# A gated linear-attention decoder block on eight cores: decay moved from k to the state, the gate pipeline started earlier, a weight scaled in slices, and another order for the last token block

## The chip, the cores and the metric

The kernel runs on the 8 cores of one Trainium2 chip. Each core computes one of the 8 batch entries with its own copy of all weights; the cores do not exchange data. The metric is the device time in microseconds of the slowest core.

Each core has a matrix engine (TensorE, PE in the profile, its weight loads PEld), a vector engine (VectorE, DVE), an activation engine (ScalarE, ACT), a general engine (GpSimd, POOL) and a queue engine (SyncE, SP). Every engine works through its own list of instructions strictly in the order of that list. It goes on to the next one when the semaphores that this one waits for have been raised.

## The reference

For x of 2048 tokens by 1024 channels per core:

```python
h = x @ W_in            # split: q 512 | k 512 | v 1024 | g 1024 | a_low 16 | u 1024 | z 1024 | gate_a 1024 | gate_b 1024
# branch A: gated linear attention, 4 heads, key width 128, value width 256
log_a = log_sigmoid(a_low @ w_gate_up + b_gate) / 16
S_t = diag(a_t) S_{t-1} + k_t^T v_t ;  o_t = q_t S_t        # computed chunk by chunk
y_a = rms_norm_per_head(o) * gn_w * silu(g)
# branch B: causal trailing means over 2, 4, 8, 16 tokens, minus the token, a per-group linear map
y_b = (pool(u) @ pool_w + pool_b) * pool_scale * silu(z)
merged = sigmoid(gate_a) * (y_a @ W_a) + sigmoid(gate_b) * (y_b @ W_b)
out = layer_norm(2**0.25 * x + merged @ W_o) * ln_w + ln_b
```

In chunk form, with b the running sum of log_a inside a chunk of 128 tokens and b_last its last value, k enters the state as k * exp(b_last - b), and the state is multiplied by exp(b_last) from chunk to chunk.

## The kernel before

The program is written out by hand: Python calls `PE(...)`, `ACT(...)`, `DVE(...)`, `POOL(...)` append one instruction each to that engine's list, with the buffers that it reads and writes; waits follow from these buffers. So the order of the calls is the order on each engine. Activations are kept transposed (channels on the 128 partitions, tokens along the row), in four token blocks `tb` of 512. A projection group is 8 matmuls of 128x512 into one of 8 PSUM banks, which another engine then empties ("evacuates").

The stages, with their time in the profile:

1. 0 to 41 us, head: `head_group` makes q and k of token block 0 and q of block 1, 32 matmuls each, k-slice by k-slice as the weights land. `mid` hooks put other work between the k-slices: the low-rank gate input of block 0 (`al_mm`) and the first two steps `a1_pre`.
2. 41 to 82 us, fill: the other 20 groups of q and k (`proj_qk`, L409), interleaved with the gate pipeline. The 16 units u are 4 token blocks times 4 heads. `a1_pre(u)` is one gate matmul (L369) and Exp and Ln on ACT (L372, L374). `a1_scan(u)` is a running sum over a chunk on DVE (L378). `a1_cum(u)` is three Exp on ACT (L385, L387, L389), which give exp(b), exp(-b) and exp(b_last), the last of these named `eblast`. When the four units of a block are done, `finalize_one` multiplies q by exp(b) and k by exp(-b) in place on DVE (L446, L448), and on POOL k by `eblast` into a second array `kdT` (L450). `drain_fin` issues one such unit at a time.
3. 82 to 248 us, attention: 32 iterations n, that is 16 chunks c times 2 head pairs hp. Between projection groups of v and g (`proj_vg`, L533, which use the two banks 2 and 3 in turn) stand the steps of the chunk: `st_T1S` (transposes of `kdT`, L549, and scores, L554), `st_UO1` (the chunk's contribution to the state, L571, and the output inside the chunk, L576), `st_O2` (output from the state, L588), `st_state` (DVE updates the state in float32, L604, and ACT makes a bfloat16 copy, L607), `st_sq` (sums of squares on ACT and POOL), `st_y` (DVE, L627), `st_Y` (transposes, L638). The queue of `drain_fin` goes on in the first iterations. At n = 8 `scale_w` multiplies the weight `wa0` by a column factor, one DVE instruction over 128x4096 (L258); at three later places it does so for `wa1`, `wb0` and `wb1`.
4. 248 to 464 us: gate a with W_a (`gate_piece`, L663 and L671), the pooling branch (L755, L797, scans on DVE), z (L838).
5. 464 to 639 us, last stage: `d_piece(g, dc)` makes one 128-channel piece of gate b with W_b for a token group g (matmuls L899 and L907, Sigmoid on ACT L903, product and sum on DVE L911, L913). `e_half` makes half of a 128-token tile of the output product (8 matmuls, L954), adds the residual on DVE with a row sum (L963), and takes the sum of squares on ACT (L969). Mean and variance are then made by small DVE instructions (L980, L982, L987) and one power on POOL (L990), and two DVE passes over 128x1024 (`n1` L996, `n2` L1003) normalise. The token groups are 512, 512, 512, 384 and 128; the pieces of the 128-token group are done in pairs (`d_pair`, L935). The list `order` sets how pieces and tiles follow one another; tile 15 is written out by hand after it.

SP issues the loads of x and the stores of the output; POOL issues the weight loads.

Of the kernel before, what the change touches and what calls it, by code (L numbers as in the profile page):

```python
# [7 lines left out]
F32 = mybir.dt.float32  # L8
# [127 lines left out]
def build_program():  # L136
# [35 lines left out]
    with ExitStack() as es:  # L172
# [157 lines left out]
        kdT = A4[:, 0:8192].rearrange("p (h t) -> p h t", h=4)  # L330
# [11 lines left out]
        b_kdb = [[Buf() for _ in range(4)] for _ in range(4)]  # L342
# [132 lines left out]

        head_group(0, 0, 1, 0, mid={4: al0_a, 7: al0_b})
        head_group(1, 0, 0, 4, mid={1: pre01})
        head_group(0, 1, 0, 0)
        al_blk(1)
        fill = [(kind, h, tb) for kind, tb in ((1, 1), (0, 2), (1, 2), (0, 3), (1, 3)) for h in range(4)]  # L480
        for u in range(NT):
# [5 lines left out]
            if u % 4 == 0:  # L487
# [3 lines left out]
            drain_fin(1)  # L491
# [3 lines left out]
        drain_fin(1)  # L495
# [47 lines left out]
        def st_T1S(n):  # L543
# [49 lines left out]
        def st_state(n):  # L593
# [4 lines left out]
            for j in range(2):  # L598
# [92 lines left out]
        for n in range(NS):  # L691
# [21 lines left out]
            if n == 8:  # L713
                scale_w(wa0, cols16[:, 0:8])
# [6 lines left out]
        if True:  # L721
# [7 lines left out]
            st_y(NS - 1)  # L729
            st_Y(NS - 2)  # L730
# [124 lines left out]
        if True:  # L855
# [16 lines left out]
            st = [(small2, small)[s // 2][:, (s % 2) * 16:(s % 2 + 1) * 16] for s in range(NSL)]  # L872
            Q = [slice(i * 256, (i + 1) * 256) for i in range(4)]
# [5 lines left out]
            groups = [(0, 512), (512, 512), (1024, 512), (1536, 384), (1920, 128)]  # L879
# [37 lines left out]
            def ld_xr(t):  # L917
                s = t % 3
                P.add("sp", lambda e: e.dma_start(out=xt[s], in_=x[t * 128:(t + 1) * 128, :]),
                      writes=b_xt[s], lane=f"xt{s}", extra=lasts)  # L920

            N_, V_, R_ = 8, 9, 10

            def d_pair(p):
                s = sctr[0] % 2
                sctr[0] += 1
                o, n = groups[4]
                banks = [next_bank(), next_bank()]
                for i in range(2):
                    for a in range(2):  # L930
                        m = (2 * p + a) % 4
                        W, wB = (gbw, wbw)[i][p // 2]
                        for k in range(KC):
                            rhs = xT[:, 3, k, 384:512] if i == 0 else szT[:, k, o:o + n]
                            PE(lambda e, i=i, a=a, m=m, W=W, k=k, rhs=rhs: e.matmul(  # L935
                                pb[banks[i]][:, a * 128:(a + 1) * 128], W[:, k, m * 128:(m + 1) * 128], rhs,
                                start=(k == 0), stop=(k == KC - 1)),
                               r=[wB] + ([b_sz[k][3]] if i else []), w=[bb[banks[i]]])
                    if i == 0:
                        ACT(lambda e: e.activation(sgm[s][:, 0:256], pb[banks[0]][:, 0:256], AF.Sigmoid),  # L940
                            r=[bb[banks[0]]], w=[b_sgm[s]])
                DVE(lambda e: e.tensor_tensor(tmpf[s][:, 0:256], pb[banks[1]][:, 0:256], sgm[s][:, 0:256], ALU.mult),
                    r=[bb[banks[1]], b_sgm[s]], w=[b_tmpf[s]])
                dst = maT[:, 2 * p:2 * p + 2, o:o + n]
                DVE(lambda e: e.tensor_tensor(dst, tmpf[s][:, 0:256].rearrange("p (a t) -> p a t", a=2), dst, ALU.add),
                    r=[b_tmpf[s]], w=b_mg[4][2 * p:2 * p + 2])

# [218 lines left out]
```

How the kernel before makes its waits and increments, by code:

```python
    def replay(self, eng_name, eng, sems):  # L108
        waited = {}
        for op in self.ops[eng_name]:
            need = {}
            for d in op.deps:
                if need.get(d.lane, 0) < d.ticket:
                    need[d.lane] = d.ticket
            for lane, val in need.items():
                if waited.get(lane, 0) < val:
                    eng.wait_ge(sems[lane], val)
                    waited[lane] = val
            ins = op.fn(eng)
            if op.sig:
                assert ins is not None
                ins.then_inc(sems[op.lane], 16 if op.is_dma else 1)
```

## Time and profile before

| | us |
|---|---|
| median of 3 runs | 640.21 (639.96 to 640.48) |
| the profiled execution | 640.21 |
| its span on the slowest core, core 4 | 638.7 |
| PE busy | 612.0 (96%), 3207 matmul records |
| DVE busy | 368.0 (58%) |
| ACT busy | 246.6 (39%) |
| POOL busy | 86.0 (13%) |

The profiled execution lasted 1.51 us longer than the span of its slowest core, and it equals the median of the runs. The chain of work that ended last lies on PE for 88% of the span, on DVE for 5%. PE's duration of a matmul includes its latency, so consecutive matmuls overlap; what a group costs is read from the start of one group to the start of the next.

### The profile page before, as it was taken

Reading aid. Unit: us, or ns where it says so; the run is one execution under the profiler, and the core shown is the slowest. Engines: PE = TensorE matmul, PEld = TensorE weight load, DVE = VectorE, ACT = ScalarE, POOL = GpSimd, SP = SyncE. Lnnn points to the kernel's source line nnn. Section 1 sums busy time; section 2 is a strip of 40 time slices with the busy share of each in tenths; the row PEclk is TensorE's granted clock in tenths of the full one; section 3 lists DMA queues with packets and bytes.
Section 4 is the critical chain, followed back from the end, with each engine's and each line's share of the span. In section 5 each row is a group of like instructions: output and inputs, shape, how many; then the busy total and the mean of one; then the engine's idle time right before and its main releaser. Section 6 shows DMA issues by size and latency. Waiting matters only on the chain.

```text
span 638.7 us, 9893 instructions; the slowest of 8 cores (635.6 to 638.7 us)
## 1 busy us (share of the span) xinstructions
PE 612.0 (96%) x3207; PEld 301.3 (47%) x3268; DVE 368.0 (58%) x621; ACT 246.6 (39%) x560; POOL 86.0 (13%) x141
## 2 busy tenths in 40 slices
PE   5999979999999999899999999999999999999995
PEld 1344335555555554444445544444444444445553
DVE  0148966676565642242123598394934666667787
ACT  0348955656656663211112433433331222222233
POOL 9003552132211212000000000001000000000010
PEclk7999989999999999999999999999999999999998
DMA  7999526000000001946102100005953113233342
GB/s 111 173 168 169 90 33 102 1 1 2 1 2 2 2 1 30 154 82 104 29 1 30 37 2 1 1 0 91 164 112 131 67 66 133 81 117 132 112 154 99
DMA packets 11569, 44.43 MB, mean 70 GB/s; under 512 B 1792, under 2 KB 2560, under 8 KB 8960
## 3 DMA queue, kind: packets, MB, share of 16 engines
q0 software_dynamic: 5904, 25.89, 25.2%
q1 hardware_dynamic: 5472, 17.65, 8.0%
q8 instruction: 27, 0.44, 0.3%
q14 instruction: 22, 0.18, 0.1%
q10 hardware_dynamic: 144, 0.26, 0.1%
HBM read 61.30 MB, written 8.39 MB: 109 GB/s over the span
## 4 chain that ended last, share of the span: by engine, by line
PE 88%; DVE 5%; issue 3%; DMA 3%; POOL 1%; ACT 0%; DVEq 0%; ACTq 0%; POOLq 0%
PE pb L533 16%; PE pb L663 9%; PE pb L838 9%; PE pb L671 9%; PE pb L797 9%; PE pb L954 9%; PE pb L899 8%; PE pb L907 8%; PE pb L409 3%; DMA ws<-head 3%; PE pb L430 2%; DVE A L378 1%; PE pb L935 1%; PE pb L755 1%; PE pb L576 1%
## 5 line engine op out<-in xcount | busy, mean ns | idle before, releaser
L533 PE MATMUL pb<-A,xT 128*128 128x512 bf16 x368 | 88.8, 385 | 2.8 <-DVE A L537 2.0
L676 DVE TENSOR_TENSOR A<-pb,sgm_t 128x512 bf16<-128x512 f32 x32 | 22.1, 691 | 85.8 <-PE pb L671 73.3
L663 PE MATMUL pb<-xT,ws 128*128 128x512 bf16 x251 | 60.0, 379 | 0.3
L899 PE MATMUL pb<-xT,ws 128*128 128x512 bf16 (+1 forms) x255 | 57.0, 366 | 0.1
L907 PE MATMUL pb<-A 128*128 128x512 bf16 (+1 forms) x252 | 56.7, 366 | 0.2
L838 PE MATMUL pb<-xT,ws 128*128 128x512 bf16 x251 | 55.2, 379 | 0.3
L797 PE MATMUL pb<-xT,A 128*128 128x512 bf16 x250 | 54.9, 379 | 0.3
L533 PEld LDWEIGHTS pb<-A,xT 128*128 128x128 bf16 x384 | 36.6, 99 | 38.8 <-issue 4.6
L667 ACT ACTIVATE sgm_t<-pb 128x512 f32<-128x512 f32 x32 | 19.1, 597 | 79.1 <-PE pb L663 75.9
L969 ACT ACTIVATE junk<-A 128x512 bf16<-128x512 f32 (+1 forms) x33 | 20.3, 615 | 69.7 <-DVE A L963 69.7
L838 PEld LDWEIGHTS pb<-xT,ws 128*128 128x128 bf16 x256 | 25.0, 98 | 30.2
L797 PEld LDWEIGHTS pb<-xT,A 128*128 128x128 bf16 x256 | 25.0, 98 | 30.0
L663 PEld LDWEIGHTS pb<-xT,ws 128*128 128x128 bf16 x256 | 24.9, 98 | 28.9
L911 DVE TENSOR_TENSOR A<-pb,sgm_t 128x512 f32<-128x512 f32 (+1 forms) x32 | 21.1, 658 | 30.3 <-PE pb L907 27.4
L899 PEld LDWEIGHTS pb<-xT,ws 128*128 128x128 bf16 x256 | 25.0, 98 | 27.3
L903 ACT ACTIVATE sgm_t<-pb 128x512 f32<-128x512 f32 (+1 forms) x32 | 18.2, 569 | 51.0 <-PE pb L899 50.0
L907 PEld LDWEIGHTS pb<-A 128*128 128x128 bf16 x256 | 25.1, 98 | 26.8
L409 PE MATMUL pb<-xT,ws 128*128 128x512 bf16 x156 | 36.8, 379 | 0.4 <-issue 0.3
L813 DVE TENSOR_TENSOR_SCAN xt<-A,small 128x2046 bf16<-128x2046 bf16 (+3 forms) x8 | 35.8, 4469 | 0.9
L537 DVE CAST A<-pb 128x512 bf16<-128x512 f32 x32 | 21.9, 685 | 20.7 <-PE pb L571 20.5
L607 ACT CAST A<-A 128x512 bf16<-128x512 f32 x30 | 18.6, 619 | 39.5 <-DVE A L604 36.6
L627 DVE SCALAR_TENSOR_TENSOR A<-pb,small,A 128x256 bf16<-128x256 f32 x64 | 30.7, 480 | 4.5 <-ACT A L607 0.8
(130 smaller groups left out, 958.6 us busy)
## 6 DMA issues: line engine op xcount, KB each, us to landing
ws<-wts POOLq DMA_DIRECT2D x9, 1024.0 KB, 11.8
A<-wts POOLq DMA_DIRECT2D x9, 1024.0 KB, 23.4
out<-A SPq DMA_DIRECT2D x15, 512.0 KB, 2.9
A<-x SPq DMA_DIRECT2D x11, 512.0 KB, 4.2
xt<-x SPq DMA_DIRECT2D x5, 512.0 KB, 4.2
xT<-xt POOLq DMA_DIRECT2D x2, 1024.0 KB, 32.3
xT<-head POOLq DMA_DIRECT2D x7, 256.0 KB, 20.3
ws<-head POOLq DMA_DIRECT2D x7, 256.0 KB, 16.1
```

The costliest lines, as they stand in the source:

```text
L409: PE(lambda e, k=k: e.matmul(pb[bank][:, :], W[:, k, h * 128:(h + 1) * 128], xTb(tb, k), start=(k == 0), stop=(k == KC - 1)), r=[WB[k], b_ ...
L533: PE(lambda e, k=k, c=c, bank=bank, W=W: e.matmul(pb[bank][:, :], xTc(c, k), W[:, k, :], start=(k == 0), stop=(k == KC - 1)), r=[B], w=[bb ...
L627: DVE(lambda e, s=s, j=j, h=h, slot=slot, y3=n % 3: e.scalar_tensor_tensor(yb_s[y3][:, j, :], pb[s][:, j * 256:(j + 1) * 256], rs_s[s][:, ...
L663: PE(lambda e, k=k, m=m, tb=tb, bank=bank, gWa=gWa: e.matmul(pb[bank][:, :], gWa[:, k, m * 128:(m + 1) * 128], xTb(tb, k), start=(k == 0), ...
L671: PE(lambda e, k=k, m=m, tb=tb, bank2=bank2, wWa=wWa: e.matmul(pb[bank2][:, :], wWa[:, k, m * 128:(m + 1) * 128], actT[:, k, tb * 512:(tb ...
L676: DVE(lambda e, s=s, dc=dc, tb=tb, bank2=bank2: e.tensor_tensor(maT[:, dc, tb * 512:(tb + 1) * 512], pb[bank2][:, :], sgm[s], ALU.mult), r ...
L797: last_u_mm[0] = PE(lambda e, k=k, m=m, tb=tb, bank=bank, uW=uW: e.matmul(pb[bank][:, :], uW[:, k, m * 128:(m + 1) * 128], xTb(tb, k), sta ...
L813: DVE(lambda e, uc=uc, w=w: e.tensor_tensor_scan(S_t[:, w:T], uc[:, w:T], uc[:, 0:T - w], sini, ALU.add, ALU.subtract), r=[b_uT[cc], b_sin ...
L838: PE(lambda e, k=k, m=m, tb=tb, bank=bank, zW=zW: e.matmul(pb[bank][:, :], zW[:, k, m * 128:(m + 1) * 128], xTb(tb, k), start=(k == 0), st ...
L899: PE(lambda e, k=k: e.matmul(pb[bank][:, 0:n], gW[:, k, m * 128:(m + 1) * 128], xT[:, tb, k, lo:lo + n], start=(k == 0), stop=(k == KC - 1 ...
L907: PE(lambda e, k=k: e.matmul(pb[bank2][:, 0:n], wW[:, k, m * 128:(m + 1) * 128], szT[:, k, o:o + n], start=(k == 0), stop=(k == KC - 1)), ...
L954: PE(lambda e, k=k: e.matmul(pb[bank][:, 0:n], maT[:, k, t * 128:(t + 1) * 128], oW[:, k, lo:lo + n], start=(k == 0), stop=(k == KC - 1)), ...
```

## The change

- **State.** `kdT` and its 16 POOL multiplications (L450) are gone. The transposes read the finished k (k times exp(-b)) itself. The stored float32 state is now the one before the chunk's decay: it is multiplied by `eblast` of the chunk before when the new contribution is added (same two DVE instructions). The bfloat16 copy that the outputs use is multiplied by `eblast` of its own chunk, in two ACT instructions of 128x256 in place of one copy of 128x512.
- **Gate pipeline.** The scans and Exp of units 0 to 3, and `a1_pre` of units 2 and 3, are issued from the `mid` hooks of the second and third head group. In the fill, one projection is done first, then the loop runs over units 4 to 15, with the remaining projections spread over these. Only 8 of the 16 `finalize_one` are issued in the fill; the other 8 follow one per iteration in n = 0 to 7. A one-element Silu on ACT ends the fill.
- **Scale.** `scale_w` is 8 DVE instructions of 128x512 with one factor per partition each. For `wa0`, 4 of them are issued at n = 8 and 4 at n = 9.
- **End of the attention.** The last `st_y` and the `st_Y` before the last are issued between the two gate pieces that follow the loop, in place of after both.
- **Last stage.** The token groups are 512, 512, 512, 256, 256, all done by `d_piece`. For tiles 0 to 13 the statistics are 7 small POOL instructions (`e_stats`), the normalisation is one ACT pass (`e_norm_act`, Identity with bias and scale), then two DVE passes multiply by ln_w and add ln_b (`e_fin`). Tiles 14 and 15 both stand behind the last piece, with statistics on DVE and ACT. `rr` has 6 slots, two of them for tiles 14 and 15 alone.

```diff
-        def scale_w(wt, cols):
+        def scale_w(wt, cols, ks=range(KC)):
             W, B = wt
-            DVE(lambda e, W=W, cols=cols: e.tensor_tensor(
-                W, W, cols.unsqueeze(2).broadcast_to([128, KC, 512]), ALU.mult),
+            for k in ks:
+                DVE(lambda e, k=k: e.tensor_scalar(W[:, k, :], W[:, k, :], cols[:, k:k + 1], None, ALU.mult),
...
-            POOL(lambda e: e.tensor_tensor(
-                kdT[:, h, sl].rearrange("p (c t) -> p c t", c=4),
...
         head_group(0, 0, 1, 0, mid={4: al0_a, 7: al0_b})
-        head_group(1, 0, 0, 4, mid={1: pre01})
-        head_group(0, 1, 0, 0)
+        head_group(1, 0, 0, 4, mid={1: pre01, 5: gs0})
+        head_group(0, 1, 0, 0, mid={1: gs1, 4: lambda: gate_step(2), 6: lambda: gate_step(3)})
...
-        for u in range(NT):
+        proj_qk(*fill.pop(0))
+        a1_pre(4)
+        a1_pre(5)
+        fin_pending += [(0, h) for h in range(4)]
+        for u in range(4, NT):
...
-            if u % 4 == 0:
+            if u % 3 != 0 and u != 7:
                 proj_qk(*fill.pop(0))
...
-            drain_fin(1)
+            if u < 12:
+                drain_fin(1)
...
-            ACT(lambda e, c=c, hp=hp: e.copy(Sbf_s[hp][(c + 1) % 2], S_f[hp]), ...
+            for j in range(2):
+                h = hp * 2 + j
+                ACT(lambda e, j=j, h=h: e.activation(
+                    Sbf_s[hp][(c + 1) % 2][:, j, :], S_f[hp][:, j, :], AF.Copy, scale=eblast[:, c, h:h + 1]),
...
-            st_y(NS - 1)
-            st_Y(NS - 2)
+                if tb == 1:
+                    st_y(NS - 1)
+                    st_Y(NS - 2)
...
+            def e_stats(t):
+                s = eslot(t)
+                POOL(lambda e: e.tensor_tensor(st[s][:, 4:6], st[s][:, 0:4:2], st[s][:, 1:4:2], ALU.add),
...
+            def e_norm_act(t):
+                s = eslot(t)
+                ACT(lambda e: e.activation(rr[s], rr[s], AF.Identity, bias=st[s][:, 7:8], scale=st[s][:, 5:6]),
...
+            def e_fin(t):
+                s = eslot(t)
+                DVE(lambda e: e.tensor_tensor(rr[s], rr[s], lnw_t, ALU.mult), r=[b_ln], w=b_rr[s])
+                DVE(lambda e: e.tensor_tensor(rr[s], rr[s], lnb_t, ALU.add), r=[b_ln], w=b_rr[s])
+                e_out(t)
...
+                     (N, 10), 11, (F, 10), (3, 7), (4, 0), (N, 11), 12, (F, 11), (4, 1), (4, 2), (N, 12),
+                     13, (F, 12), (4, 3), (4, 4), (N, 13), (4, 5), (F, 13), (4, 6), (4, 7)]
...
+            e_half(14, 0)
+            e_half(14, 1)
+            e_mean(14)
+            n1(14)
+            e_half(15, 0)
+            e_rcp(14)
+            n2(14)
+            e_out(14)
+            e_half(15, 1)
```

The list of `d_piece`, tile, (N, t) and (F, t) entries above is in the order of issue: a tuple of numbers is a piece, a bare number a tile, N the ACT pass, F the two DVE passes and the store.

On DVE, at the end of the head, before (L420 evacuates the head groups, L378 is the scan, L355 the gate input, L395 a k group):

```order
L472 TENSOR_SCALAR nbg<-colsT 128x4
L420 TENSOR_SCALAR A<-pb 128x512 x4
L355 CAST A<-pb 128x512
L378 SCALAR_TENSOR_TENSOR A<-mask_t,A 128x512
L395 CAST A<-pb 128x512
L378 SCALAR_TENSOR_TENSOR A<-mask_t,A 128x512
```

and in the changed kernel (L418, L376, L353 and L393 are the same four lines):

```order
L465 TENSOR_SCALAR nbg<-colsT 128x4
L376 SCALAR_TENSOR_TENSOR A<-mask_t,A 128x512
L418 TENSOR_SCALAR A<-pb 128x512 x2
L376 SCALAR_TENSOR_TENSOR A<-mask_t,A 128x512 x3
L418 TENSOR_SCALAR A<-pb 128x512 x2
L353 CAST A<-pb 128x512
L393 CAST A<-pb 128x512
L376 SCALAR_TENSOR_TENSOR A<-mask_t,A 128x512
```

Four scans have moved ahead of the last evacuations of the head.

On DVE, at the end of the fill and the start of the attention, before (L446 and L448 are `finalize_one`, L537 the evacuation of v, L560 the masked scores):

```order
L378 SCALAR_TENSOR_TENSOR A<-mask_t,A 128x512
L395 CAST A<-pb 128x512
L446 TENSOR_TENSOR A<-A 128x512
L448 TENSOR_TENSOR A<-A 128x512
L378 SCALAR_TENSOR_TENSOR A<-mask_t,A 128x512
L446 TENSOR_TENSOR A<-A 128x512
L448 TENSOR_TENSOR A<-A 128x512
L446 TENSOR_TENSOR A<-A 128x512
L448 TENSOR_TENSOR A<-A 128x512
L537 CAST A<-pb 128x512 x2
L560 TENSOR_TENSOR A<-pb,lt 128x256
```

and in the changed kernel (L393, L396 evacuations of k and q, L547 of v, L570 the scores):

```order
L376 SCALAR_TENSOR_TENSOR A<-mask_t,A 128x512
L396 TENSOR_SCALAR A<-pb 128x512
L376 SCALAR_TENSOR_TENSOR A<-mask_t,A 128x512
L396 TENSOR_SCALAR A<-pb 128x512
L393 CAST A<-pb 128x512
L376 SCALAR_TENSOR_TENSOR A<-mask_t,A 128x512
L393 CAST A<-pb 128x512
L376 SCALAR_TENSOR_TENSOR A<-mask_t,A 128x512
L547 CAST A<-pb 128x512 x2
L570 TENSOR_TENSOR A<-pb,lt 128x256
```

The products of `finalize_one` are gone from this place; between the last scan and the first evacuation of v stands nothing.

On ACT, at the end of the program, before (L969 squares of a tile, L940 Sigmoid of a pair, L1058 and L1078 square roots):

```order
L969 ACTIVATE junk,small<-A 128x512 x2
L940 ACTIVATE sgm_t<-pb 128x256
L969 ACTIVATE junk,small<-A 128x512 x2
L940 ACTIVATE sgm_t<-pb 128x256 x2
L1058 ACTIVATE small<-cpow 128x1
L969 ACTIVATE junk,small<-A 128x512
L969 ACTIVATE junk,small<-A 128x256 x2
L1078 ACTIVATE small<-small 128x1
L1010 DMA out<-A 128x512
```

and in the changed kernel (L957 squares, L919 Sigmoid of a piece, L980 the normalising pass, L1051 and L997 square roots):

```order
L957 ACTIVATE junk,small<-A 128x512 x2
L919 ACTIVATE sgm_t<-pb 128x256 x2
L980 ACTIVATE A<-A,small 128x1024
L919 ACTIVATE sgm_t<-pb 128x256 x3
L1051 ACTIVATE small<-cpow 128x1
L957 ACTIVATE junk,small<-A 128x512 x2
L997 ACTIVATE small<-small 128x1
L957 ACTIVATE junk,small<-A 128x512 x2
L997 ACTIVATE small<-small 128x1
L1021 DMA out<-A 128x512
```

The Sigmoid of the last three pieces stands behind the normalising pass of tile 13.

## Rows read from the trace of the kernel before

**Rows 1.** Span and granted clock of the slowest core.
```profile
core 4: 638.7 us, clock 0.985
```
**Rows 2.** Core 4: stretch, us; busy PE, PEld, DVE, ACT, POOL; clock, DMA, GB/s.
```profile
60.00:82.20 22.20, 20.99 (x100) 8.83 (x99) 22.20 (x34) 20.87 (x46) 13.11 (x8) 1.00 0.57 93
82.20:95.00 12.80, 8.89 (x35) 3.69 (x37) 8.01 (x12) 5.94 (x11) 6.71 (x6) 0.87 0.24 35
```
**Rows 3.** Timeline, fill to attention: start, us, engine, line, count, [idle before].
```profile
40.73 0.61 PE L350 MATMUL pb<-xT,wal_s 128*32 128x512 bf16 x8
...
50.93 0.68 ACT L372 ACTIVATE A<-pb,nbg 128x512 f32<-128x512 f32 x1
...
51.20 1.89 PE L409 MATMUL pb<-xT,ws 128*128 128x512 bf16 x8
...
52.93 0.38 PE L369 MATMUL pb<-A,wg_s 128*128 128x512 bf16 x1
...
53.37 0.67 ACT L372 ACTIVATE A<-pb,nbg 128x512 f32<-128x512 f32 x1
...
54.96 0.61 PE L350 MATMUL pb<-xT,wal_s 128*32 128x512 bf16 x8
...
55.74 1.67 PE L409 MATMUL pb<-xT,ws 128*128 128x512 bf16 x7 [0.16 <-issue]
...
78.57 3.62 PE L409 MATMUL pb<-xT,ws 128*128 128x512 bf16 x16
...
84.07 1.89 PE L533 MATMUL pb<-ws,xT 128*128 128x512 bf16 x8 [1.88 <-DVE A L395]
...
89.67 5.08 PE L533 MATMUL pb<-A,xT 128*128 128x512 bf16 x15 [1.99 <-DVE A L537]
...
94.81 0.28 PE L549 MATMUL pb<-ident,A 128*128 128x128 bf16 x2
```
**Rows 4.** Timeline, scale at n = 8, and after the attention loop.
```profile
132.91 0.20 POOL L616 TENSOR_TENSOR small<-small,cpow 128x2 f32<-128x2 f32 x1 [4.01 <-ACT A L613]
...
133.25 0.69 POOL L618 TENSOR_TENSOR small<-small,cpow 128x2 f32<-128x2 f32 x1
...
136.14 4.41 DVE L258 TENSOR_TENSOR ws<-ws,cols 128x4096 bf16<-128x4096 bf16 x1
...
136.87 0.38 PE L571 MATMUL pb<-A 128*128 128x256 bf16 x2
...
136.98 3.63 POOL L616 TENSOR_TENSOR small<-small,cpow 128x2 f32<-128x2 f32 x1 [3.04 <-ACT A L613]
...
142.00 0.38 PE L571 MATMUL pb<-A 128*128 128x256 bf16 x2 [0.42 <-DVE A L604]
...
147.36 0.38 PE L571 MATMUL pb<-A 128*128 128x256 bf16 x2
...
254.88 0.39 PE L638 MATMUL pb<-ident,A 128*128 128x128 bf16 x4
...
257.07 0.38 PE L638 MATMUL pb<-ident,A 128*128 128x128 bf16 x4 [1.81 <-DVE A L627]
```
**Rows 5.** Timeline, the end.
```profile
627.54 1.24 PE L954 MATMUL pb<-A 128*128 128x512 bf16 x5
...
634.61 1.41 DVE L1003 SCALAR_TENSOR_TENSOR A<-A,small 128x512 f32<-128x512 f32 x2
```
**Rows 6.** Groups by line and shape: busy us, mean ns | idle before.
```profile
L378 DVE TENSOR_TENSOR_SCAN A<-mask_t,A 128x512 f32<-128x512 f32 x16 | 20.6, 1288 | 0.1
...
L844 DVE TENSOR_TENSOR A<-A 128x512 bf16<-128x512 bf16 x32 | 11.2, 416 | 1.4 <-ACT A L841 1.3
...
L963 DVE SCALAR_TENSOR_TENSOR A<-A,pb 128x512 f32<-128x512 f32 x21 | 14.3, 687 | 11.3 <-PE pb L954 11.3
...
L1003 DVE SCALAR_TENSOR_TENSOR A<-A,small 128x1024 f32<-128x1024 f32 x10 | 12.8, 1280 | 0.0
...
L945 DVE TENSOR_TENSOR A<-A 128x256 bf16<-128x256 f32 x4 | 1.7, 426 | 0.4
```

More of the change, by code:

```diff
@@ L494, in build_program @@
         assert not fill
-        drain_fin(1)
+        ACT(lambda e: e.activation(small[:, 60:61], cpow[:, 6:7], AF.Silu), r=[b_cpow])
         NVS = 2
@@ L919, in ld_xr @@
                 P.add("sp", lambda e: e.dma_start(out=xt[s], in_=x[t * 128:(t + 1) * 128, :]),
[L920 to L946, printed above, removed]
@@ L948, in e_mm, with eslot, e_half @@
[L948 to L953 removed]
+                      writes=[b_xt[s]], lane=f"xt{s}", extra=lasts)
+            def eslot(t):
+                return t % 4 if t < NT - 2 else 4 + t % 2
+            def e_half(t, half):
+                s = eslot(t)
+                g = t // 4 if t < 12 else 3 + (t - 12) // 2
+                bank = next_bank()
+                oW, oB = wow[half]
+                for k in range(KC):
@@ new lines, in e_rcp, with n1 @@
+            def e_rcp(t):
+                s = eslot(t)
+                DVE(lambda e: e.reciprocal(st[s][:, 5:6], st[s][:, 5:6]), w=[b_st[s][6]])
+            def n1(t, hs=slice(0, D)):
+                s = eslot(t)
+                hb = b_rr[s] if hs.stop - hs.start == D else [b_rr[s][hs.start // 512]]
+                DVE(lambda e: e.scalar_tensor_tensor(
+                    rr[s][:, hs], rr[s][:, hs], st[s][:, 4:5], lnw_t[:, hs], ALU.add, ALU.mult),
+                    r=[b_st[s][4], b_ln], w=hb)
@@ new lines, in n2, with e_out @@
+            def n2(t, hs=slice(0, D)):
+                s = eslot(t)
+                hb = b_rr[s] if hs.stop - hs.start == D else [b_rr[s][hs.start // 512]]
+                DVE(lambda e: e.scalar_tensor_tensor(
+                    rr[s][:, hs], rr[s][:, hs], st[s][:, 5:6], lnb_t[:, hs], ALU.mult, ALU.add),
+                    r=[b_st[s][6], b_ln], w=hb)
+            def e_out(t, half=None, eng="sp"):
+                s = eslot(t)
+                hs = slice(0, D) if half is None else H[half]
@@ L1078, in build_program @@
-            ACT(lambda e: e.activation(st[s][:, 12:13], st[s][:, V_:V_ + 1], AF.Sqrt, bias=st[s][:, 7:8], scale=-1.0),
-                r=[b_st[s][7], b_st[s][V_]], w=[b_st[s][12]])
-            n1(t, 0, 2)
-            n1(t, 2, 4)
-            DVE(lambda e: e.reciprocal(st[s][:, R_:R_ + 1], st[s][:, 12:13]), r=[b_st[s][12]], w=[b_st[s][R_]])
+            ACT(lambda e: e.activation(small[:, 56:57], cpow[:, 6:7], AF.Sqrt), r=[b_cpow])
+            e_half(14, 0)
+            e_half(14, 1)
+            e_mean(14)
```

184 lines of the change are left out of this document (70 added, 114 removed).

## The prediction, made before the changed kernel was run

> **What bounds the kernel now.** I read the page of the profile first: PE is busy for 96% of the span, so the change can only win where PE stands still, and the share of each engine over the whole run says nothing more. Then the spans of the cores: the slowest is core 4, at a mean granted clock of 0.985 [rows 1]. Then the timeline of PE of that core, looking for bracketed waits, and the same stretches on the other engines.
>
> PE waits in four places that the change touches. In the fill (41 to 82 us) DVE is busy 22.20 of 22.20 us, while PE is not full [rows 2]: the gate pipeline sets the pace. At the end of the fill PE waits twice for DVE evacuations that are queued behind scans and products, 1.88 and 1.99 us, and the matmuls after the second wait run slowly: granted clock 0.87 over that stretch [rows 2, 3], that is, some of it at 1.2 GHz and the rest at 2.4. Behind the 4.41 us scale of n = 8 two iterations come late, and after the attention loop 1.81 us for the last `st_y` [rows 4]. From there to the end of the last stage PE is full. The end itself lasts from the last 128-token pair, at 627.54, to the end of the span at 638.7: 11.16 us [rows 1, 5].
>
> The sum is made against the profiled execution, 640.21 us, which is 1.51 us above its span of 638.7 and equals the median of the runs shown.
>
> **Fill and junction.** What would PE need without waiting? A projection group takes 52.93 - 51.20 = 1.73 us from start to start, a gate matmul 0.215 (an eighth of it), the low-rank block between the second and third token block 55.74 - 54.96 = 0.78 [rows 3], and the first such block 0.55 by the same timeline. In the changed kernel the stretch begins with the low-rank block at 40.73 + 0.43, since two gate matmuls more stand in the head. Then 0.55 + 20 x 1.73 + 12 x 0.215 + 2 x 0.78 = 39.3 us, which ends at 80.4. Before, it ended at 78.57 + 2 x 1.73 = 82.0, so 1.6 us were lost inside. Then came the waits, from 82.0 to 84.07 (2.05 us) and from 87.5 to 89.67 (2.15 us), and the last two groups took 94.81 - 89.67 = 5.14 us for 3.45, 1.7 us more at the lower clock. Sum 1.6 + 2.05 + 2.15 + 1.7 = 7.5 us: the first transpose moves from 94.81 to 87.3.
>
> Does the pipeline keep up? ACT needs 53.37 - 50.93 = 2.44 us per unit [rows 3]; with 12 units from 43.7 (when the block-1 gate input is there) and 6 evacuations of at most 0.68, it is done by 77.1 if it never waits, 3 us before PE. DVE has 12 scans of 1.29 [rows 6], 16 evacuations of at most 0.69 and 8 pairs of products at 2 x 0.42: 33 us out of 39, against 16 scans and 14 pairs before; the POOL products that shared memory with it are gone as well. After unit 11 no products stand between scans and evacuations, and 3 PSUM banks of slack cover 5 us of delay. In the head the early scans and Exp stand ahead of evacuations; walked through in order with the durations above, ACT ends its head evacuations about 0.6 us later than now, and PE needs those banks only after another group of 1.73 us. That is nothing; if the cover fails, PE waits the 0.6 us there.
>
> The 8 products that move to n = 0 to 7 add 0.8 us to DVE per iteration. An iteration on PE is two groups and 2560 columns of small matmuls, which cost five times 0.215: 4.53 us; and before, n = 0 and 1 carried their products without a PE wait. Of the state, the two ACT copies with a factor cost at most 2 x 0.68 for one copy, off the path because the next reader is two iterations later. The POOL products (L450) were on no path of PE. Nothing for both.
>
> **Scale.** The trace has no 128x512 instruction with a factor per partition in bfloat16. From below it is free, from above it costs 0.69 as the float evacuations do; I take 0.42, the row of the same size and type [rows 6]. Four at n = 8 hold the queue for 1.7 us in place of 4.41, less than the 4.41 - 1.4 = 3.0 us of the old instruction that PE did not feel, so the waits go; at the upper bound 2.8 us they would just go too. From L571 to L571 the two iterations took 147.36 - 136.87 = 10.5 us for 2 x 4.53: gain 1.4. (VectorE: DVE Perf Modes of the Trainium skill, section on the perf-mode tier table, gives 693 ns for such an instruction of 2048 elements, which would make it some 0.3 us as an estimate; the sum is the same.)
>
> **End of the attention.** The last `st_y` moves behind the first gate piece, and the pair of groups of the second piece, 3.45 us, covers its two DVE instructions and the sums it waits for; PE loses nothing more. Gain 257.07 - 254.88 - 0.22 = 2.0 us.
>
> Gains together 7.5 + 1.4 + 2.0 = 10.9 us.
>
> **Last stage.** PE's work is the same: 256-wide, 384-wide and 128-wide matmuls cost their columns; the old split needed about 0.3 us more. DVE's load per tile stays alike (two passes of 1.28). What is new is a loop through three engines: the ACT pass of a tile, then the squares of the next, its 7 POOL instructions, its ACT pass. A small POOL instruction takes 0.34 from start to start, a power 0.69 [rows 4]: 2.75 us. But POOL waits for DVE: the one L616 that started inside the 4.41 us product of two arrays in SBUF took 3.63 instead of 0.20, until that product had ended [rows 4]. The new DVE passes have two such inputs each, and they run just when the statistics are due. GPSIMD Engine Reference of the Trainium skill, Key points, says the same: its memory interface is contended by DVE instructions with two inputs in SBUF. By that rule, the trace agrees, POOL is held.
>
> While the groups are 512 wide, a tile and two pieces last 10.36 us on PE and the loop about 7.2 held (squares 1.5, rest of the DVE passes 1.0, POOL 2.75 with two adds of 0.43 in between, ACT pass 1.1): no cost. An ACT pass of 1024 is bounded by 0.68 and 1.36; I take 1.1. At 256 wide, the PE time is 6.9, the loop falls behind, and this decides the end.
>
> Let T be the end of the last piece. Tile 13 ends at T - 8.65. The ACT pass of tile 12 ends at -7.6, the squares of 13 at -6.2; the DVE passes of tile 12 hold POOL until -5.1; its seven instructions, held twice by adds, end at -2.1; the ACT pass of 13 at -0.9. Only then come the Sigmoids of the last three pieces. DVE then does piece 5 (until +0.35), the two passes of tile 13 (until +2.85), piece 6 (+3.7) and piece 7 (+4.5). Tile 14 needs piece 7 for its eighth matmul: its first half ends at +4.8 in place of +1.73, a PE wait of 3.1 us. From there DVE is the path: residual of the second half at +6.8, then 0.8, three small ones of 0.34, pass 1.28, residual of tile 15 0.7, reciprocal 0.3, pass 1.28, residual 0.8, small ones 1.0, two half passes 1.4, reciprocal 0.3, less some 0.5 where starts overlap: 8.4; then as before 638.7 - 634.61 = 4.1 from the last two half passes to the end [rows 1, 5]. The end is T + 19.3. Before it was 11.16 after 627.54, and T lies 3.45 + 0.3 before that point, because tile 14 now stands behind the pieces. Loss 19.3 - 3.75 - 11.16 = 4.4 us.
>
> Sum: 640.2 - 10.9 + 4.4 = 633.7 us.
>
> **The rivals.**
>
> POOL not held. For it: it is one instruction of 3.63 that I judge by, and the passes are float32. Then the statistics end 1.3 us earlier per tile, tile 14 is stalled only 1.1 us, the loss is 2.4 and the time 631.7.
>
> The fill stays bound. Against it: the sums above leave ACT 3 us and DVE 6 us. For it: waits of ACT on DVE and back were not counted, and ACT was already at 20.87 of 22.20 [rows 2]. If ACT is what is late at the end, half of the 7.5 us stays: 637.5.
>
> The loop through ACT, DVE and POOL becomes the bound of the whole last stage, and the kernel gets slower. Per tile it must exceed 10.36 us, from a held 7.2. Every POOL instruction held once by a 0.69 us add would make it 7 x (0.34 + 0.69) = 7.2 in POOL alone, 11.7 in all: 1.3 us x 12 tiles = 16 us, time 650. It decides from a loop of about 10.9, where 0.5 us per tile eats the gain of 6.5. Against it: DVE has idle stretches between pieces, in which POOL can go on. A table load before each ACT pass and after it would add 2.6 us, 9.8 in all: still hidden, but 2.6 us more at the end, 636.3.
>
> The early scans cost in the head what they save in the fill (ACT in front of the head's evacuations), so that the change does not do what it says: 2 us lost of the 10.9, about 636.
>
> **How the numbers follow.** Forecast 633.7 with chance 0.60 (its own range 632.3 to 635.5: a lower clock after the 3 us wait would cost up to 1.7); POOL not held 0.15; fill still bound or head late, 636 to 637.5, 0.15; slower or no gain through the loop 0.10. A measurement of this kernel can tell 0.2% (1.3 us) from no change. All but the last are faster: 0.88 after a little for the unforeseen; within 0.2%: 0.04; slower 0.08. The range 630.8 to 637.2 leaves out the slow case and little on either side.
>
> **What would show it.** Right: the first transpose of the attention near 87.3 with granted clock 1.00 from 80 to 100 us; no PE wait at n = 8 to 10 nor at the last `st_Y`; a PE wait of 2 to 4 us in the first half of tile 14, ended by DVE; about 19 us from the end of the last piece to the end of the span. Wrong: PE waits for ACT or DVE between 45 and 80 us, or in each tile of the last stage; POOL instructions at 0.2 beside the DVE passes.

## The result and the profile after

The changed kernel takes 635.87 us (median; three runs lie between 635.59 and 636.05), the kernel before 640.35 on the same chip: ratio 0.9929 (95% interval 0.9909 to 0.9948). A fourth run took 757.34 us, with the cores of one die at a clock near 0.81; such runs, here and below, count in the medians and not in the ratios. The gain is 4.5 us; the forecast was 6.5 us and 633.7. The profiled execution took 636.05 us; its slowest core is again core 4. The busy times on its page:

```profile
PE 612.8 (97%) x3200; PEld 306.5 (48%) x3260; DVE 349.8 (55%) x614; ACT 273.1 (43%) x608; POOL 92.8 (15%) x207
```

PE has the same work as before and waits less. All its waits on core 4 (engine and line, what ended them: us in total, times, longest):

```profile
PE pb L428 <- DMA ws<-head: 4.7, 2, 2.8
PE pb L947 <- DVE A L929: 2.4, 2, 2.0
PE pb L320 <- DVE warm L307: 1.9, 1, 1.9
PE pb L428 <- DVE A L353: 0.4, 1, 0.4
PE pb L428 <- issue: 0.2, 1, 0.2
```

L428 and L320 are the head, where the weights land; they waited before too. Nothing is left of the waits in the fill, behind the scale and after the attention. New is L947, the first half of tile 14. The timeline of PE from the end of the fill to the attention, which answers to [rows 3]:

```profile
74.34 7.07 PE L407 MATMUL pb<-xT,ws 128*128 128x512 bf16 x31
81.25 1.89 PE L543 MATMUL pb<-ws,xT 128*128 128x512 bf16 x8
82.97 5.34 PE L543 MATMUL pb<-A,xT 128*128 128x512 bf16 x23
88.15 0.28 PE L559 MATMUL pb<-ident,A 128*128 128x128 bf16 x2
```

Four groups of v and g in 88.15 - 81.25 = 6.90 us, 1.73 each: no wait and the full clock. At n = 8, which answers to [rows 4]:

```profile
129.52 1.73 DVE L259 TENSOR_SCALAR ws<-ws,cols 128x512 bf16<-128x512 bf16 x4
...
130.22 0.38 PE L581 MATMUL pb<-A 128*128 128x256 bf16 x2
...
133.45 1.73 DVE L259 TENSOR_SCALAR ws<-ws,cols 128x512 bf16<-128x512 bf16 x4
...
134.77 0.38 PE L581 MATMUL pb<-A 128*128 128x256 bf16 x2
...
139.32 0.38 PE L581 MATMUL pb<-A 128*128 128x256 bf16 x2
```

From L581 to L581 it is 4.55 us both times, as in every other iteration. The end of the program, which answers to [rows 5], on the engines of the loop (L963 to L975 are the statistics of tile 13 on POOL, L980 is its normalising pass on ACT; L985 and L986 are the two DVE passes of a tile, at 607.53 of tile 12 and from 613.92 of tile 13; L919 are Sigmoids, L927 and L929 the product and the sum of a piece on DVE):

```profile
607.25 0.23 POOL L963 TENSOR_TENSOR small<-small 128x2 f32<-128x2 f32 x1 [2.98 <-ACT junk L957]
607.53 1.23 DVE L986 TENSOR_TENSOR A<-A 128x1024 f32<-128x1024 f32 x1
607.62 1.19 POOL L965 TENSOR_TENSOR small<-small,cpow 128x2 f32<-128x2 f32 x1
...
608.95 0.19 POOL L967 TENSOR_TENSOR small<-small 128x1 f32<-128x1 f32 x1
...
611.03 0.19 POOL L975 TENSOR_TENSOR small<-small 128x1 f32<-128x1 f32 x1
611.37 1.24 ACT L980 ACTIVATE A<-A,small 128x1024 f32<-128x1024 f32 x1 [2.78 <-POOL small L975]
...
612.52 0.64 ACT L919 ACTIVATE sgm_t<-pb 128x256 f32<-128x256 f32 x2
...
613.92 1.22 DVE L985 TENSOR_TENSOR A<-A 128x1024 f32<-128x1024 f32 x1
...
614.27 1.24 PE L947 MATMUL pb<-A 128*128 128x512 bf16 x5
615.24 1.22 DVE L986 TENSOR_TENSOR A<-A 128x1024 f32<-128x1024 f32 x1
...
616.39 0.42 DVE L927 TENSOR_TENSOR A<-pb,sgm_t 128x256 f32<-128x256 f32 x1
...
617.48 0.38 PE L947 MATMUL pb<-A 128*128 128x512 bf16 x1 [1.96 <-DVE A L929]
...
618.34 0.59 PE L947 MATMUL pb<-A 128*128 128x512 bf16 x1 [0.49 <-DVE A L929]
618.72 3.33 PE L947 MATMUL pb<-ws,A 128*128 128x512 bf16 x8
...
621.89 1.89 PE L947 MATMUL pb<-A 128*128 128x512 bf16 x8
```

L965 takes 1.19 us where its like took 0.20 [rows 4]: it ends at 608.81, just after the DVE pass L986 at 608.76. The statistics last from 607.25 to 611.22; the pass of tile 13 ends at 612.61, and only then come the Sigmoids of the last three pieces. Those of the last two end at 613.16 and 614.01, but on DVE the two passes of tile 13, which had waited for the ACT pass, stand in front of these pieces until 616.46; their products start at 616.39 and 617.25. For these two pieces PE waits in tile 14, and the next eight matmuls take 621.89 - 618.72 = 3.17 us for 1.73: the clock fell to its lower level for them (granted 0.54 between 618.7 and 621.9).

The time of core 4 in both profiles, cut at four points. The end of the pieces is 614.27 after; before it is put at 627.54 less the 3.45 us of tile 14, which now stands behind the pieces:

| stretch | before | after | gained | forecast |
|---|---|---|---|---|
| start to the end of the 0.4 us wait in the head | 26.62 | 27.30 | -0.7 | 0 |
| to the first transpose | 68.19 | 60.85 | 7.3 | 7.5 |
| to the end of the pieces | 529.28 | 526.12 | 3.2 | 3.7 |
| to the end of the span | 14.61 | 20.03 | -5.4 | -4.7 |
| span | 638.7 | 634.3 | 4.4 | 6.5 |

(The forecast's 0.3 for the old split stands here in the third row, not in the fourth. The rows at 614.27 and at 627.54 have 5 matmuls, where most other cores have 6 in this place: the list lacks the first one, and both points lie 0.2 us earlier. The differences stay.)

### The profile page after: what moved, and what is told of

Read it like the earlier page. It is cut to its first block, busy times and chain, and to the rows that moved or that the text cites. A ratio compares the mean times of both kernels' runs of the same rounds, so it can differ in the third digit from the quotient of the medians.

```text
span 634.3 us, 10082 instructions; the slowest of 8 cores (630.4 to 634.3 us)
## 1 busy us (share of the span) xinstructions
PE 612.8 (97%) x3200; PEld 306.5 (48%) x3260; DVE 349.8 (55%) x614; ACT 273.1 (43%) x608; POOL 92.8 (15%) x207
## 4 chain that ended last, share of the span: by engine, by line
PE 94%; DMA 2%; DVE 2%; issue 1%; POOL 1%; DVEq 0%; ACT 0%; ACTq 0%; POOLq 0%
PE pb L543 17%; PE pb L677 9%; PE pb L685 9%; PE pb L853 9%; PE pb L812 9%; PE pb L915 9%; PE pb L923 9%; PE pb L947 8%; PE pb L407 5%; PE pb L428 3%; DMA ws<-head 2%; PE pb L652 1%; PE pb L581 1%; PE pb L770 1%; PE pb L586 1%
## 5 line engine op out<-in xcount | busy, mean ns | idle before, releaser
L543 PE MATMUL pb<-A,xT 128*128 128x512 bf16 x368 | 87.1, 379 | 0.8
L915 PE MATMUL pb<-xT,ws 128*128 128x512 bf16 (+1 forms) x319 | 61.9, 336 | 0.1
L923 PE MATMUL pb<-A 128*128 128x512 bf16 (+1 forms) x316 | 61.6, 336 | 0.2
L619 ACT ACTIVATE A<-A,eblast 128x256 bf16<-128x256 f32 x60 | 30.5, 508 | 40.2 <-DVE A L614 35.0
L927 DVE TENSOR_TENSOR A<-pb,sgm_t 128x512 f32<-128x512 f32 (+1 forms) x40 | 23.3, 582 | 39.4 <-PE pb L923 32.3
L915 PEld LDWEIGHTS pb<-xT,ws 128*128 128x128 bf16 x320 | 31.3, 98 | 25.6
L923 PEld LDWEIGHTS pb<-A 128*128 128x128 bf16 x320 | 31.3, 98 | 24.1
L919 ACT ACTIVATE sgm_t<-pb 128x512 f32<-128x512 f32 (+1 forms) x40 | 20.2, 508 | 50.9 <-PE pb L915 50.4
L853 PEld LDWEIGHTS pb<-xT,ws 128*128 128x128 bf16 x256 | 25.0, 98 | 30.2
L677 PEld LDWEIGHTS pb<-xT,ws 128*128 128x128 bf16 x256 | 24.9, 98 | 28.8 <-issue 0.2
L957 ACT ACTIVATE junk<-A 128x512 bf16<-128x512 f32 x32 | 20.1, 628 | 40.1 <-DVE A L951 38.0
L815 ACT CAST A<-pb 128x512 bf16<-128x512 f32 x32 | 18.7, 585 | 37.0 <-PE pb L812 37.0
L547 DVE CAST A<-pb 128x512 bf16<-128x512 f32 x32 | 21.9, 686 | 22.3 <-PE pb L581 19.7
## 6 DMA issues: line engine op xcount, KB each, us to landing
ws<-wts POOLq DMA_DIRECT2D x9, 1024.0 KB, 10.5
```

What stands on the lines that cost most here:

```text
L543: PE(lambda e, k=k, c=c, bank=bank, W=W: e.matmul(pb[bank][:, :], xTc(c, k), W[:, k, :], start=(k == 0), stop=(k == KC - 1)), r=[B], w=[bb ...
L619: ACT(lambda e, j=j, h=h: e.activation(Sbf_s[hp][(c + 1) % 2][:, j, :], S_f[hp][:, j, :], AF.Copy, scale=eblast[:, c, h:h + 1]), r=[b_S[hp ...
L677: PE(lambda e, k=k, m=m, tb=tb, bank=bank, gWa=gWa: e.matmul(pb[bank][:, :], gWa[:, k, m * 128:(m + 1) * 128], xTb(tb, k), start=(k == 0), ...
L853: PE(lambda e, k=k, m=m, tb=tb, bank=bank, zW=zW: e.matmul(pb[bank][:, :], zW[:, k, m * 128:(m + 1) * 128], xTb(tb, k), start=(k == 0), st ...
L915: PE(lambda e, k=k: e.matmul(pb[bank][:, 0:n], gW[:, k, m * 128:(m + 1) * 128], xT[:, tb, k, lo:lo + n], start=(k == 0), stop=(k == KC - 1 ...
L923: PE(lambda e, k=k: e.matmul(pb[bank2][:, 0:n], wW[:, k, m * 128:(m + 1) * 128], szT[:, k, o:o + n], start=(k == 0), stop=(k == KC - 1)), ...
```

## The experiments

All against the kernel before, whose median was 639.98 us for the first four kernels on record (labels e1 to e4) and 640.20 for the other four, on another chip. A gain below is a difference of medians; the interval of its ratio is some 0.6 to 1.1 us to either side. The theory, that of the prediction: the fill gains because the gate pipeline starts earlier, the scale and the end of the attention lose their waits, and the last stage loses because statistics and ACT pass come late. Its rival for the fill, read from the changed profile: the state edit is part of the gain, since the POOL products it removes had held DVE.

**The four edits with the last stage of before.** The diff against the changed kernel puts back the token groups 512, 512, 512, 384, 128 and the old statistics.

```diff
-            groups = [(0, 512), (512, 512), (1024, 512), (1536, 256), (1792, 256)]
+            groups = [(0, 512), (512, 512), (1024, 512), (1536, 384), (1920, 128)]
...
-            def e_stats(t):
...
+            order += [12, (N, 12), ("pair", 0), (F, 12), 13, (N, 13), ("pair", 1), (F, 13), 14, ("pair", 2), (N, 14),
```

> The changed kernel with the last stage of the kernel before (groups of 384 and 128, statistics on DVE, tile 15 by hand): only the last stage differs from the changed kernel. Theory (the sum of the prediction): the four edits ahead of the last stage are worth 10.9 us less about 0.9 in the head, the last stage lost about 4.4 and a lower clock after the wait in tile 14 on some cores; so 630 us, some 6 us under the changed kernel, and the time from the last piece to the end back near 11 us. Rival: the last stage costs nothing and the gains ahead of it are only 4.5 us; then 635.9.

Measured: 631.17 us, ratio 0.9858 (0.9844 to 0.9872). The four edits gain 8.8 us where the whole change gains 4.5, so the new last stage costs 4.3 us (4.7 by the two medians, measured at different times; the two intervals leave some 1.5 us to either side). The profiles, from the first transpose to the end of a core's span, have 540.7 to 541.0 us here; in the changed kernel 544.4 to 545.1 on five cores, and 546.0 to 546.2 on the three whose clock fell in tile 14. This kernel is faster than both.

**The state edit alone.**

```diff
-            POOL(lambda e: e.tensor_tensor(
-                kdT[:, h, sl].rearrange("p (c t) -> p c t", c=4),
...
-                    pbT[4][:, j * 128:(j + 1) * 128], kdT[:, h, c * 128:(c + 1) * 128], ident[:]),
+                    pbT[4][:, j * 128:(j + 1) * 128], kbT[:, h, c * 128:(c + 1) * 128], ident[:]),
...
-            ACT(lambda e, c=c, hp=hp: e.copy(Sbf_s[hp][(c + 1) % 2], S_f[hp]), r=[b_S[hp]], w=[b_Sbf[hp][(c + 1) % 2]])
...
+                    Sbf_s[hp][(c + 1) % 2][:, j, :], S_f[hp][:, j, :], AF.Copy, scale=eblast[:, c, h:h + 1]),
```

> The kernel before with the state edit alone (no POOL products, the decay in the ACT copies). Theory as predicted: no path of PE held the POOL products, 640.3 within 1 us. Rival: the products hold DVE's memory interface (a DVE product took 1.20 us beside one and 0.41 without), so DVE, which was full in the fill, gets faster by about 4 us and the two waits at the end of the fill shrink or go; 635 to 637.

Measured: 635.98 us, ratio 0.9937 (0.9924 to 0.9950): 4.0 us gained by the part that was forecast at nothing. Of the two waits of 1.88 and 1.99 us, one of 0.66 is left (core 2, its slowest):

```profile
81.46 1.89 PE L526 MATMUL pb<-ws,xT 128*128 128x512 bf16 x8
84.01 5.12 PE L526 MATMUL pb<-A,xT 128*128 128x512 bf16 x23 [0.66 <-ACT A L400]
89.18 0.28 PE L542 MATMUL pb<-ident,A 128*128 128x128 bf16 x2
```

**The state edit with the POOL products kept.** Two things went with the state edit: 16 POOL products, and the transposes' wait for them. This kernel has the state edit and goes on issuing the products, into an array that nobody reads (the lines that the edit alone removes):

```diff
+            POOL(lambda e: e.tensor_tensor(
+                kdT[:, h, sl].rearrange("p (c t) -> p c t", c=4),
+                kbT[:, h, sl].rearrange("p (c t) -> p c t", c=4),
...
```

> The kernel before with the state edit, but the 16 POOL multiplications into the second array stay, and nobody reads their results. Theory (the state edit gained 4.0 us because the POOL multiplications held DVE's products in the fill): the gain is gone, DVE products take up to 1.2 us again, PE waits twice at the end of the fill, time 639 to 640.4. Rival (the gain comes from the transposes, which no longer wait for POOL): the gain stays, about 636.

Measured: 641.0 us, ratio 1.0012 (1.0003 to 1.0021): the whole gain is gone. (The kernel is even 0.8 us slower than the one before; why, no run shows.) PE waits twice again at the end of the fill, on every core, and the groups of `finalize_one` (busy us, mean ns) are, on core 1, its slowest:

```profile
PE pb L533 <- DVE A L537: 2.0, 1, 2.0
PE pb L533 <- DVE A L395: 1.9, 1, 1.9
...
L450 POOL TENSOR_TENSOR A<-A,eblast 128x512 bf16<-128x512 bf16 x16 | 23.6, 1476 | 59.4 <-DVE A L448 50.3 <-ACT eblast L389 5.9 <-ACT A L372 2.4
L446 DVE TENSOR_TENSOR A<-A 128x512 bf16<-128x512 bf16 x16 | 10.0, 624 | 0.0
L448 DVE TENSOR_TENSOR A<-A 128x512 bf16<-128x512 bf16 x16 | 7.5, 467 | 0.0
```

The kernel before has the same 624 and 467 ns. The state edit alone, on core 2 (L444 and L446 are the same two products):

```profile
L446 DVE TENSOR_TENSOR A<-A 128x512 bf16<-128x512 bf16 x16 | 6.7, 418 | 0.0
L444 DVE TENSOR_TENSOR A<-A 128x512 bf16<-128x512 bf16 x16 | 6.6, 413 | 0.0
```

The products cost DVE (624 + 467 - 418 - 413) x 16 = 4.2 us here, and the 16 scans take 1288 ns in place of 1219 on the same two cores, 1.1 us more. The timeline of the kernel before shows how, at the second wait:

```profile
87.31 0.41 DVE L446 TENSOR_TENSOR A<-A 128x512 bf16<-128x512 bf16 x1
87.59 1.05 POOL L450 TENSOR_TENSOR A<-A,eblast 128x512 bf16<-128x512 bf16 x1 [0.82 <-DVE A L448]
87.65 1.27 DVE L448 TENSOR_TENSOR A<-A 128x512 bf16<-128x512 bf16 x1
88.85 0.68 DVE L537 CAST A<-pb 128x512 bf16<-128x512 f32 x1
```

The POOL product began 0.06 us before L448 and kept it until 88.64; L448 took 1.27 us for 0.41, and L537, for which PE waited, stood behind it. So the hold is shown, and not only argued: with the products back, and read by nobody, the waits are back.

**The gate pipeline alone.**

```diff
-        head_group(1, 0, 0, 4, mid={1: pre01})
-        head_group(0, 1, 0, 0)
+        head_group(1, 0, 0, 4, mid={1: pre01, 5: gs0})
+        head_group(0, 1, 0, 0, mid={1: gs1, 4: lambda: gate_step(2), 6: lambda: gate_step(3)})
...
```

The rest of the edit is that of the change: the fill loop over units 4 to 15, the 8 products moved to n = 0 to 7, the Silu.

> The kernel before with the gate edit alone (early scans, products of the last 8 units moved into the attention, Silu at the end of the fill), POOL products kept. Theory: this is the whole of the 7.5 us; first transpose near 87.3 plus what the head adds, granted clock 1.00 from 80 to 100 us, 633 us. Rival: without the state edit the POOL products still hold DVE; the fill stays late by 2 to 4 us and the time is 635 to 637.

Measured: 633.68 us, ratio 0.9903 (0.9887 to 0.9918), 6.3 us gained, though the POOL products are all there. The waits of the fill are gone on every core, as after the whole change.

**Without the state edit.** Gate pipeline, scale and end of the attention, the last stage of before.

> The kernel before with three parts: gate pipeline, scale and end of the attention, without the state edit and with the last stage of before. Theory (state edit and gate pipeline remove the same fill waits, so that one of them is enough): the same time as with the state edit, 631.2, within 0.7 us. Rival (the state edit is worth its 4 us, or a part of it, beside the gate pipeline as well): 632.5 to 635.

Measured: 630.99 us, ratio 0.9856 (0.9839 to 0.9872), the same as with the state edit (631.17, 0.9858). Behind the head neither of the two has a PE wait on any core. The stretch from the end of the 0.4 us wait in the head to the first transpose, read on all cores, leaves out where the head began and says the same:

| kernel | us from there to the first transpose |
|---|---|
| before | 66.5 on four cores, 68.2 on the four whose clock fell |
| state edit alone | 62.1 on all |
| state edit with the POOL products | 66.5 on four cores, 68.2 on four |
| gate pipeline alone | 60.85 on all |
| gate pipeline, scale and end of the attention | 60.85 on all |
| the changed kernel | 60.85 on all |

So the two edits remove the same waits, and beside the gate pipeline the state edit is worth nothing that can be measured. This kernel too is faster than both.

**The scale alone, and the end of the attention alone.**

```diff
...
-                W, W, cols.unsqueeze(2).broadcast_to([128, KC, 512]), ALU.mult),
+            DVE(lambda e, k=k: e.tensor_scalar(W[:, k, :], W[:, k, :], cols[:, k:k + 1], None, ALU.mult),
...
```

> The kernel before with the scale in 8 instructions of 128x512 (4 at n = 8, 4 at n = 9) and nothing else of the change. In the changed kernel one of them took 0.35 us, so four hold DVE's queue for 1.4 us in place of 4.41. Theory: both PE waits behind the scale go, the two iterations take 9.1 in place of 10.5 us: 1.4 us less, 638.6. Rival: the waits are shorter than the spacing says and the time lost comes back in later iterations: less than 0.7 us, no difference that can be told.

Measured: 638.51 us, ratio 0.9972 (0.9963 to 0.9982): 1.7 us gained, and no PE wait behind the scale is left.

```diff
-            st_y(NS - 1)
-            st_Y(NS - 2)
+                if tb == 1:
+                    st_y(NS - 1)
+                    st_Y(NS - 2)
```

> The kernel before with only the last output scaling and the last transpose but one moved between the two gate pieces that follow the loop. Theory: the PE wait of 1.81 us goes, with the spacing 2.0 us: 638.0. Rival: what stands in its place is late too (the DVE products of the moved step stand in front of what the second piece needs) and a wait of 0.5 to 1 us remains: 639 to 639.5.

Measured: 638.16 us, ratio 0.9967 (0.9954 to 0.9979): 2.0 us gained; nothing waits in its place.

**The changed kernel with tile 13 later.** The ACT pass of tile 13 stands behind the Sigmoids of the last pieces, its two DVE passes behind the first half of tile 14.

```diff
-                     13, (F, 12), (4, 3), (4, 4), (N, 13), (4, 5), (F, 13), (4, 6), (4, 7)]
+                     13, (F, 12), (4, 3), (4, 4), (4, 5), (4, 6), (4, 7), (N, 13)]
...
             e_half(14, 0)
+            e_fin(13)
             e_half(14, 1)
```

> The changed kernel with the ACT pass of tile 13 behind the last three Sigmoids, and its two DVE passes behind the residual of the first half of tile 14. Theory: the PE wait of 2.4 us in tile 14 came from the Sigmoids queued behind that pass; it goes, and with it the lower clock after it; DVE then has the two passes of tile 13 as its only extra, 2.5 us, where it would have waited; 632 to 633.5 us. Rival: the end is bound by DVE's sum of work, wherever the wait lies; 635 to 636.

Measured: 632.83 us, ratio 0.9885 (0.9871 to 0.9899), 7.2 us gained where the changed kernel gains 4.5: 2.7 us (3.0 by the two medians). Tiles 14 and 15 on PE and the ACT pass of tile 13, core 7:

```profile
611.49 1.23 ACT L980 ACTIVATE A<-A,small 128x1024 f32<-128x1024 f32 x1
611.82 1.89 PE L947 MATMUL pb<-A 128*128 128x512 bf16 x8
613.54 1.89 PE L947 MATMUL pb<-ws,A 128*128 128x512 bf16 x8
615.27 1.89 PE L947 MATMUL pb<-A 128*128 128x512 bf16 x8
617.00 1.89 PE L947 MATMUL pb<-ws,A 128*128 128x512 bf16 x8
```

No wait and 1.73 us from half to half, here and on the other seven cores. The wait and what followed it came from the place of tile 13's passes. This kernel moves the ACT pass and the two DVE passes together; which of the two moves would have been enough was not tried. The rows of the changed kernel speak for the DVE passes: the products of the last two pieces start there 3.2 us after their Sigmoids have ended. The 1.7 us that remain to the kernel with the old last stage belong to the longer end: from the last piece to the end of the span it is 628.9 - 611.82 = 17.1 us here, and 627.5 - 612.86 = 14.6 with the old last stage (core 0, tile 14 counted as in the table above). Its parts were not tried apart.

## Why the prediction was right, and where it was off

The direction and the four places were right, and so was the place of the loss. The time lies in the wide range of the forecast, 0.4 us outside its own narrow one. By its steps:

- **Fill and junction**, 7.5 forecast. On core 4 it was 7.3, the first transpose at 88.15 for 87.3, of which 0.68 is the later start of the head. Within it one term was too small: a gate matmul in the head costs more than an eighth of a group. Two of them were to cost 0.43; from the wait in the head to the first group of the fill it became 0.85 longer (14.66 to 15.51 us, on all cores). Such a matmul has 32 rows (wg_s 32x512), where those of the fill after the change have 128 and take 0.215: the next one starts 32.54 - 32.22 = 0.32 us behind it, and the 16 ahead of the second one take 36.10 - 32.54 = 3.56 us for 3.45 (core 5, below; the list of core 4 lacks a matmul here). The profile of before had a row of this kind, 43.43 - 43.11 = 0.32 us. Another term was too large, by a misread row: the 0.78 us of the low-rank block, 55.74 - 54.96, end at a group of 7 matmuls [rows 3], whose first is missing from the list; core 0 has all 8, and 0.54 us. By this the fill was forecast some 0.5 us too long; it took 81.25 - 42.26 = 38.99 us for 39.3.

  As a gain of the kernel the term was too large: 6.3 us for this edit alone. The 1.7 us of lower clock are in the sum for core 4, but in the profile of before cores 1, 2, 5 and 6 had the same waits without it (from the first group of the fill to the first transpose 51.84 us, against 53.5 on cores 0, 3, 4 and 7; 45.34 on all cores after). The low-rank block before, core 0, and the two gate matmuls in the head after the change, core 5:

```profile
54.38 0.61 PE L350 MATMUL pb<-xT,wal_s 128*32 128x512 bf16 x8
54.92 1.90 PE L409 MATMUL pb<-xT,ws 128*128 128x512 bf16 x8
```
```profile
32.22 0.39 PE L367 MATMUL pb<-A,wg_s 32*128 32x512 bf16 x1
32.54 3.63 PE L428 MATMUL pb<-xT,ws 128*128 128x512 bf16 x16
36.10 0.39 PE L367 MATMUL pb<-A,wg_s 32*128 32x512 bf16 x1
36.42 5.35 PE L428 MATMUL pb<-xT,ws 128*128 128x512 bf16 x24
```

- **State, "nothing for both".** This step failed. It said that the POOL products were on no path of PE. They were, through DVE: the prediction weighed that DVE holds POOL, and not that POOL holds DVE, though the means of L446 and L448 in the profile of before, 624 and 467 ns, stood beside the 416 of L844 [rows 6]. Alone the edit gains 4.0 us. That the sum did not suffer is luck, as far as this reason goes: the gate pipeline removes the same waits. (SBUF — State Buffer of the Trainium skill, section SBUF: two separate sides, says it in both directions: whichever of the two starts first has the shared ports for its whole instruction, and the other stands still. By that rule, L448 at 1.27 us, the trace agrees.)
- **Scale**, 1.4 forecast: 4.55 us per iteration in the profile after, 10.5 - 9.1 = 1.4; alone 1.7 (four instructions were to hold the queue for 1.7 us and take 1.73; the mean of one is 0.35, for the 0.42 taken). **End of the attention**, 2.0 forecast: 2.0.
- **Products moved to n = 0 to 7, early scans in the head**, nothing: no PE wait came of them.
- **The last stage**, a loss of 4.4: by the run with the old last stage 4.3, or 4.7 by the medians. The chain came as worked out: POOL held (3.97 us for the statistics, 4.1 forecast), ACT pass, Sigmoids, DVE passes, PE (2.4 us of wait, 3.1 forecast). The end of the first half of tile 14 was at +4.7 us from the end of the pieces (the missing matmul counted), +4.8 forecast. What the sum left out is the lower clock after that wait: 3.17 us for eight matmuls in place of 1.73. It was named as a possibility with up to 1.7. Without it the end is 18.8 us, for 19.3. Two small slips in the sum cancel: the old split had no 0.3 us more on PE (8 x 2 x 1.30 + 8 x 0.89 = 27.9 us before, 16 x 2 x 0.87 = 27.9 after), and the 11.16 us from 627.54 are 11.4 with the missing matmul.
- **What separates 633.7 from 635.87.** On core 4 the head began 0.7 us later (between cores it varies by 2.3 us after, 24.99 to 27.30), the lower clock cost 1.4, the split 0.3, and two small remainders (junction, loop) 0.2 each; the rest of the end came out 0.7 better, 0.2 of it from the missing matmul. That is 2.1 us, the distance between 6.5 and 4.4. That core 4 is the slowest is the meeting of the first two: core 5 had a late head (26.74) and no lower clock, and ended at 632.0. By the runs the miss lies elsewhere: the edits ahead of the last stage gained 8.8 us (9.2 without the state edit) in place of 10.9, and the loss was 4.3, as forecast. The sum had counted 1.7 us of lower clock, which four cores of before don't show, as a gain of the kernel. That the loss came out so close is in part luck: the end behind the pieces was shorter than worked out, and the lower clock of three cores, which was not in the sum, filled the gap.

Of the rivals, POOL not held is refuted by L965; the fill is not bound; the loop of ACT, DVE and POOL stays behind PE until the 256-token groups. That the early scans cost something in the head holds for 0.42 us, on PE itself and not through ACT.

## What to carry to other kernels

An instruction on an idle engine can be on the path through what it does to its neighbour: compare the mean duration of an operation in the stretch in question with the same operation elsewhere, and read a longer one as a wait that no list of waits shows. Two edits that remove the same wait don't add up: the state edit gained 4.0 us alone and the gate pipeline 6.3, but beside the second the first gained nothing and could have been left out. At the end of a program, what stands ahead of the last small pieces on ACT and DVE decides: the three passes of one tile, put behind them, were worth some 3 us.

## What the runs showed of the hardware

The hold between DVE and POOL works in both directions and lasts until the instruction that came first has ended: POOL L965 1.19 us for 0.20 behind a DVE pass, DVE L448 1.27 us for 0.41 behind a POOL product. PSUM evacuations were not held in the kernel before: L537 took 0.69 us at 89.70 beside the POOL product from 89.13 to 90.18, and L395 0.66 at 83.26 beside the one from 82.41 to 84.18.

A wait of the same length does not lower the clock on every core. In the kernel before it fell behind the waits of 1.88 and 1.99 us on cores 0, 3, 4 and 7, and with the state edit and its products on 0, 1, 5 and 7. Two cores after the change, both with waits of 1.96 and 0.49 us in tile 14 (stretch, us; busy PE, PEld, DVE, ACT, POOL; clock, DMA, GB/s; core 4 first, then core 5):

```profile
612.00:620.00 8.00, 5.50 (x31) 3.01 (x30) 5.43 (x10) 3.20 (x7) 0.00 (x0) 0.89 0.17 69
620.00:626.00 6.00, 5.50 (x22) 2.16 (x20) 3.40 (x10) 1.79 (x6) 0.00 (x0) 0.86 0.00 0
```
```profile
612.00:620.00 8.00, 5.55 (x34) 2.99 (x32) 5.43 (x11) 3.19 (x8) 0.00 (x0) 1.00 0.16 66
620.00:626.00 6.00, 3.34 (x16) 1.31 (x14) 5.37 (x13) 2.05 (x6) 0.00 (x0) 1.00 0.00 0
```

From the first transpose to the start of the last eight matmuls cores 3, 4 and 6 took 535.4 to 535.5 us, the other five 533.86: only those three fell to the lower level there. What makes the difference stays open; so a time of the slowest of 8 cores has to reckon with it after such waits.
